# Stage b of an eight-stage float32 kernel: gate tiles taken earlier, output product with own banks, norm sums behind the first unit

## What is computed

```python
def mixer_b(h, w_in, q_gain, k_gain, w_out):        # h = rms_norm(x, g)
    proj = h @ w_in                                 # 3 patterns x (q, k, v), and z
    for g, (window, dilation) in enumerate(B_PATTERNS):
        q = apply_partial_rotary(rms_norm(qkv[:, :, 0, g], q_gain[g]), cos, sin)
        k = apply_partial_rotary(rms_norm(qkv[:, :, 1, g], k_gain[g]), cos, sin)
        o, lse = dilated_window_attention(q, k, qkv[:, :, 2, g], window // dilation, dilation)
    wgt = jax.nn.softmax(jnp.stack(lses), axis=0)
    o = jnp.einsum('gbsh,gbshd->bshd', wgt, jnp.stack(outs))
    y = o.reshape(bsz, S, B_WIDTH).astype(h.dtype) * jax.nn.silu(z)
    return y @ w_out                                # then x = x + y, and stage c begins
```

## Time and profile before

| | us |
|---|---|
| median of 3 runs | 3117.05 (3115.99 to 3117.53) |
| the profiled execution, whole | 3117.01 |
| its span, first to last instruction | 3115.2 |
| TensorE busy in it (matmul) | 2932.7 |
| VectorE busy | 1777.0 |
| ScalarE busy | 1082.4 |
| mean granted TensorE clock | 0.965 of full speed |

### The profile page before, as it was taken

The page is one execution under the profiler, slowest core; times in us unless marked ns, Lnnn a source line. Parts: engine busy times, 40 slices in busy tenths (PEclk is TensorE's granted clock), DMA queues, the critical chain, the costliest instruction groups (busy, mean ns, idle before and its releaser), DMA issues.

```text
span 3115.2 us, 38431 instructions
## 1 busy us (share of the span) xinstructions
PE 2932.7 (94%) x14024; PEld 2409.4 (77%) x14024; DVE 1777.0 (57%) x2641; ACT 1082.4 (35%) x1602; POOL 268.7 (9%) x247
## 2 busy tenths in 40 slices
PE   8999999999999899999999978699999868899998
PEld 6888888877888678878888856598888744788887
DVE  5555536763676466654545587655444578464445
ACT  4332324442444332233322444443222423442222
POOL 1000000000000000000000061220000533110001
PEclk9999999999999899999999989699999879999999
DMA  3322232212211233333232311023333210123332
GB/s 142 104 92 88 92 104 69 61 55 80 69 62 55 62 95 100 96 95 94 89 97 92 102 61 48 7 83 111 93 100 96 80 34 14 48 88 95 100 96 88
DMA packets 70400, 252.12 MB, mean 81 GB/s; under 512 B 7808, under 2 KB 9856, under 8 KB 69632
## 3 DMA queue, kind: packets, MB, share of 16 engines
q1 hardware_dynamic: 68112, 241.89, 25.0%
q10 hardware_dynamic: 2160, 8.49, 0.8%
HBM read 248.25 MB, written 2.10 MB: 80 GB/s over the span
## 4 chain that ended last, share of the span: by engine, by line
PE 77%; DVE 11%; issue 5%; ACT 3%; POOL 3%; DMA 0%; DVEq 0%; ACTq 0%; POOLq 0%
PE ps L296 17%; PE ps L297 17%; PE ps L298 17%; PE ps L570 2%; PE ps L571 2%; PE ps L572 2%; DVE w_low L283 2%; ACT w_high L276 2%; POOL arena L2014 1%; PE ps L781 1%; PE ps L783 1%; PE ps L782 1%; PE ps L854 1%; PE ps L593 1%; PE ps L840 1%
## 5 line engine op out<-in xcount | busy, mean ns | idle before, releaser
L283 DVE TENSOR_TENSOR w_low<-raw,w_high 128x1024 fp32r<-128x1024 f32 x456 | 567.0, 1248 | 417.6 <-ACT w_high L276 410.8
L296 PE MATMUL ps<-h_high,w_high 128*128 128x512 f32 x1872 | 738.0, 394 | 5.7 <-DVE arena L1423 3.0
L298 PE MATMUL ps<-h_high,w_low 128*128 128x512 f32 x1872 | 730.4, 390 | 0.0
L297 PE MATMUL ps<-h_low,w_high 128*128 128x512 f32 x1872 | 730.2, 390 | 0.0
L276 ACT ACTIVATE w_high<-raw 128x1024 fp32r<-128x1024 f32 x456 | 477.5, 1050 | 428.9 <-PE ps L298 214.1
L296 PEld LDWEIGHTS ps<-h_high,w_high 128*128 128x128 f32 x1872 | 352.6, 188 | 81.1 <-issue 4.3
L298 PEld LDWEIGHTS ps<-h_high,w_low 128*128 128x128 f32 x1872 | 352.2, 188 | 73.8
L297 PEld LDWEIGHTS ps<-h_low,w_high 128*128 128x128 f32 x1872 | 352.6, 188 | 69.9
L296 PE MATMUL ps<-y_high,w_high 128*128 128x512 f32 x656 | 258.6, 394 | 8.0 <-DVE x L520 4.3
L297 PE MATMUL ps<-y_low,w_high 128*128 128x512 f32 x656 | 257.2, 392 | 0.0
L298 PE MATMUL ps<-y_high,w_low 128*128 128x512 f32 x656 | 257.1, 392 | 0.0
(11 more groups left out here) (398 smaller groups left out, 4612.7 us busy)
## 6 DMA issues: line engine op xcount, KB each, us to landing
raw<-stream SPq DMA_DIRECT2D x456, 512.0 KB, 3.6
table<-tables_in ACTq DMA_DIRECT2D x5, 1088.0 KB, 7.3
x<-x_in ACTq DMA_DIRECT2D x8, 256.0 KB, 8.2
x_out<-x SPq DMA_DIRECT2D x16, 128.0 KB, 1.7
const<-const_in SPq DMA_DIRECT2D x1, 673.0 KB, 7.8
work<-ssm_in ACTq DMA_DIRECT2D x1, 512.0 KB, 3.5
params<-params_in ACTq DMA_DIRECT2D x1, 287.0 KB, 6.6
```

Source lines behind the costliest of these rows:

```text
L283: nc.vector.tensor_tensor(w_low[:, u.slot], raw[:, u.raw], w_high[:, u.slot].bitcast(F32), ALU.subtract).then_inc(weights_low, 1)
L296: nc.tensor.matmul(bank, wh, high[:, k], start=k == 0, stop=False)
L297: nc.tensor.matmul(bank, wh, low[:, k], start=False, stop=False)
L298: mm = nc.tensor.matmul(bank, wl, high[:, k], start=False, stop=k == tiles - 1)
```

## The change

The gate tile of head u is taken in slot (4, u) itself, after the block's negative maximum and ahead of the wait for the exponential (head 0's at the end of slot (4, 0)). gate is cut in three: gate (tanh + 1, ahead of that wait), gated (times the output, where gate was), low (y_low, at the head of the next slot, ahead of its split). ScalarE's tanh goes one slot up with it.

In the output product tiles 6 and 7 get banks 4 and 5, and no wait. k = 6 and k = 7 of a tile follow each other, so that tiles 0 to 3 are done one after another. VectorE's order there is written out: takes first, splits between, h_low behind. ScalarE splits unit 4 before the first square.

At the beginning of the stage norm_sums is issued behind values(0, 0, 0).

```diff
-        B_BANKS = (0, 1, 2, 3, 6, 7, 6, 7)
+        B_BANKS = (0, 1, 2, 3, 6, 7, 4, 5)
...
             pe.wait_ge(out_free, 8 * o + 2)
-            norm_sums(pe, R_PRE["b"], True)
...
                             values(i, g, kk)
+                        if (i, g, kk) == (0, 0, 0):
+                            norm_sums(pe, R_PRE["b"], True)
...
             for m in range(4):
                 out_tile(m, KD - 2)
-            for m in range(4):
                 out_tile(m, KD - 1).then_inc(units_done, 1)
             for m in range(4, KD):
-                if m >= 6:
-                    pe.wait_ge(out_free, 8 * o + m + 1)
                 product(pe, Unit(first + 2 * B_HALF + m), ps[:, B_BANKS[m]], y_high, y_low)
...
-                    if j == BH and 1 <= u <= BH:
-                        m = u - 1
-                        act.wait_ge(b_z_taken, BH * i + m + 1)
+                    if j == BH and u < BH:
+                        act.wait_ge(b_z_taken, BH * i + u + 1)
...
-                            act.wait_ge(b_gated, 2 * (BH * i + m))
+                            act.wait_ge(b_gated, 2 * (BH * i + u) - 1)
+                        nc.scalar.activation(b_tanh, b_szs[u % 2][:], ACT.Tanh, scale=0.5).then_inc(b_silu, 1)
+                    if j == BH and 1 <= u < BH:
+                        act.wait_ge(b_gated, 2 * (BH * i + u))
+                        nc.scalar.activation(y_high[:, 4 * i + u - 1], full[:, (u - 1) % 2], ACT.Copy).then_inc(y_high_done, 1)
...
+            for m in range(KD):
+                if m < KD - 1:
+                    split_high(act, Unit(first + 2 * B_HALF + m + 1 + AHEAD))
+                act.wait_ge(out_free, 8 * o + m + 3)
+                norm_square(act, r, m, x[:, m])
+                high_of(act, following, m)
...
+                    if j == BH and 2 <= u <= BH:
+                        low(u - 2)
                     if b_split_unit(first, i, j, u) is not None:
                         split_low(dve, b_split_unit(first, i, j, u) + AHEAD)
-                    if j == BH and 1 <= u <= BH:
...
                         nc.vector.tensor_scalar(b_neg, b_max, -1.0, None, op0=ALU.mult).then_inc(b_soft, 1)
+                        if j == BH and u < BH:
+                            take_z(u)
+                        if j == BH:
+                            gate(u - 1)
                         dve.wait_ge(b_exp, lin(n + 1, i, 16))
...
+                    if (j, u) == (BH, 0):
+                        take_z(0)
                     if j == BH and 1 <= u < BH:
                         dve.wait_ge(b_o_copied, lin(u, i, 3))
-                        gate(u - 1, b_o[:, u - 1])
+                        gated(u - 1, b_o[:, u - 1])
                 dve.wait_ge(b_pv, lin(16, i, 16))
-                gate(3, ps[:, 7])
+                gated(3, ps[:, 7])
+                low(3)
...
+            take(0)
+            split(4)
+            take(1)
+            take(2)
+            split(5)
+            take(3)
+            low_of(dve, following, 0)
+            low_of(dve, following, 1)
+            split(6)
+            low_of(dve, following, 2)
+            low_of(dve, following, 3)
+            split(7)
+            for m in range(4, KD):
+                take(m)
+                if m < KD - 1:
+                    split(m + 1 + AHEAD)
+                low_of(dve, following, m)
```

More of the change, by code:

```diff
@@ L488, in out_product, with out_split @@
             rounds(pe, last, body)
-        def out_split(act, o, first, target=None, r=None, last=False, following=None, split=0):
+        def out_split(act, o, first, target=None, r=None, last=False, following=None):
             def body(loop, at):
                 for j in range(4):
-                    if loop is not None or at + j >= split:
-                        split_high(act, Unit(first + at + j + AHEAD, loop, 4 if loop is not None else 0))
+                    split_high(act, Unit(first + at + j + AHEAD, loop, 4 if loop is not None else 0))
                     if r is not None:
@@ L500, in out_split, with out_take @@
             rounds(act, last or r is not None, body)
-        def out_take(dve, o, first, target, fresh=False, r=None, classes=False, last=False, following=None, split=0,
-                     banks=(6, 7, 6, 7, 6, 7, 6, 7)):
+        def out_take(dve, o, first, target, fresh=False, r=None, classes=False, last=False, following=None):
             def body(loop, at):
@@ L508, in body @@
                     u = Unit(first + at + j, loop, per)
-                    if loop is not None or at + j >= split:
-                        split_low(dve, u + AHEAD)
+                    split_low(dve, u + AHEAD)
                     if following is not None and at + j > 0:
@@ L515, in body @@
                     tile = target[:, bass.ds(m, 1)].rearrange("q a t -> q (a t)")
-                    bank = ps[:, banks[at + j]]
+                    bank = ps[:, 6 + j % 2]
                     if fresh:
@@ L938, in b_scalar @@
                         nc.scalar.activation(b_p, b_p, ACT.Exp, bias=b_neg, accum_out=b_sum).then_inc(b_exp, 1)
-                    if j == BH and 1 <= u <= BH:
-                        m = u - 1
-                        act.wait_ge(b_z_taken, BH * i + m + 1)
-                        if m == 0:
+                    if j == BH and u < BH:
+                        act.wait_ge(b_z_taken, BH * i + u + 1)
+                        if u == 0:
                             act.wait_ge(b_ss, 6 * BH * (i + 1))
                         else:
-                            act.wait_ge(b_gated, 2 * (BH * i + m))
-                        nc.scalar.activation(b_tanh, b_szs[m % 2][:], ACT.Tanh, scale=0.5).then_inc(b_silu, 1)
-                        if m < BH - 1:
-                            act.wait_ge(b_gated, 2 * (BH * i + m + 1))
-                            nc.scalar.activation(y_high[:, 4 * i + m], full[:, m % 2], ACT.Copy).then_inc(y_high_done, 1)
+                            act.wait_ge(b_gated, 2 * (BH * i + u) - 1)
[3 more added lines that the diff above has]
+                        nc.scalar.activation(y_high[:, 4 * i + u - 1], full[:, (u - 1) % 2], ACT.Copy).then_inc(y_high_done, 1)
                 act.wait_ge(b_gated, 2 * BH * (i + 1))
                 nc.scalar.activation(y_high[:, 4 * i + 3], full[:, 1], ACT.Copy).then_inc(y_high_done, 1)
-            out_split(act, o, first + 2 * B_HALF, x, r, last, following, split=1)
+            for m in range(KD):
[4 more added lines that the diff above has]
+                high_of(act, following, m)
         def b_vector(dve, first, o, y_base, r, last=False, following=None):
@@ L981, in gate, with take_z @@
                                             ALU.subtract).then_inc(y_low_done, 1)
+                def take_z(m):
+                    if i == 0:
+                        dve.wait_ge(b_r_kept, 1)
+                    if m == 0:
+                        dve.wait_ge(b_ss, lin(6 * BH - 1, i, 6 * BH))
+                    dve.wait_ge(units_done, b_unit(first, i, BH, m).count(1))
+                    nc.vector.tensor_tensor(b_szs[m % 2][:], ps[:, m], b_r[:], ALU.mult).then_inc(b_z_taken, 1)
                 for j, u in B_SLOTS:
@@ L1062, in b_vector, with take, split @@
                         nc.vector.tensor_copy(b_o[:, pv[0]], ps[:, 7]).then_inc(b_o_copied, 1)
+                    if (j, u) == (BH, 0):
+                        take_z(0)
                     if j == BH and 1 <= u < BH:
                         dve.wait_ge(b_o_copied, lin(u, i, 3))
-                        gate(u - 1, b_o[:, u - 1])
+                        gated(u - 1, b_o[:, u - 1])
                 dve.wait_ge(b_pv, lin(16, i, 16))
-                gate(3, ps[:, 7])
-            out_take(dve, o, first + 2 * B_HALF, x, r=r, classes=True, last=last, following=following, split=1, banks=B_BANKS)
+                gated(3, ps[:, 7])
+                low(3)
+            def take(m):
+                dve.wait_ge(units_done, Unit(first + 2 * B_HALF + m).count(1))
+                nc.vector.tensor_tensor(by_class(x[:, m]), by_class(x[:, m]), grouped(ps[:, B_BANKS[m]]),
+                                        ALU.add).then_inc(out_free, 1)
+            def split(m):
+                split_low(dve, Unit(first + 2 * B_HALF + m))
+            take(0)
[15 more added lines that the diff above has]
+                low_of(dve, following, m)
         def tail_tensor(pe, name, o, first, y_base, tiles=KD):
```

18 lines of the change are left out of this document (6 added, 12 removed).

## The result

| | before | after |
|---|---|---|
| median of 4 runs, us | 3116.52 (3114.34 to 3117.53) | 3093.41 (3087.44 to 3098.52) |
| profiled execution, us | 3117.01 | 3087.44 |
| its span, us | 3115.2 | 3085.6 |

The ratio is 0.9926, 95% interval 0.9907 to 0.9945: 23.1 us faster, where 3095.1 had been forecast. The profiled execution is the fastest of the four; 29.6 us lie between the two spans. The next table says where.

What follows compares the result with a forecast made beforehand. TensorE bounds the kernel (matmuls 94% of the span), so only its idle or low-clock time can be won. 0.5 + 9.6 + 2.5 + 9.3 = 21.9 us off 3117.0 gives 3095.1 us, range 3088 to 3103.

Steps and rivals of the forecast that it cites:

- Half 0: Stage b, half 0: the last gate tile's wait falls from 7.85 to about 1.1 us, full clock behind; 9.6 us gained.
- Half 1: Stage b, half 1: the wait for the last gate tile shortens to some 6 us, ended by w_low; 2.5 us gained.
- rival B: Half 1 restarts with the take as half 0 does, if w_low were ready: another 5.0 + 2.3, so 3088; chance 0.08.
- The wait's term: Half 1: TensorE restarts at 1021.6 against 1023.82, held by output tile 3's w_low; gain 2.2 us.
- The clock's term: Half 1: low clock stays behind the wait, slow stretch maybe 3.7 to 5.3 us; 0.3 us taken as gained.
- The end: End of stage b: waits of 2.60 and 4.28 us and their slow clock go, k = 7 waits 1.67; 9.3 gained.
- rival E: End of stage b: VectorE's written-out order makes splits fall behind TensorE, costing 29.9 us, so 3125; chance 0.04.
- The beginning: Start of stage b: moving the norm sums changes only the clock, one slow stretch behind them; 0.5 us gained.
- Rival C: Clock falls at new short waits (1.1 in half 0, 1.67 at end) and at the beginning: 5.4 back, 3100.5; chance 0.20.
- bad side: Start of stage b: slow stretches behind both the idle time and the norm sums, 1.7 + 2.4 against 2.6; 1.5 lost.
- Rival D: Half 0: take and gate delay the reciprocal and the round; 4 to 5 us lost, 3100; chance 0.08 with F.
- F: Gate tiles are still taken late; excluded for the order, counted into Rival D, together chance 0.08.

Runs made afterwards that it cites:

- e6: Changed kernel with output unit 3's weight split (high and low parts) moved one slot earlier in half 1, on ScalarE and VectorE; 3092.88 us.
- e8: Changed kernel with the edits of e5, e6 and e7 together; 3084.57 us, ratio 0.9901 to the kernel before.
- e7: Changed kernel with k = 6 of tiles 0 to 2 put ahead of k = 7 of tile 0; 3093.14 us.
- e3: Kernel before with only the new end of stage b (banks, k = 6 and 7 together, takes first, split and squares); 3106.55 us, ratio 0.9966.
- e4: Kernel before with only output tiles 6 and 7 given banks 4 and 5 and their wait removed; 3119.71 us, ratio 1.0009.
- e9: Changed kernel with the norm sums parted: 8 matmuls behind value unit 0, 8 behind unit 1; 3093.09 us.
- e10: Kernel before with stage b's norm column sums read in blocks of neighbouring positions instead of every fourth (norms go to wrong positions); 3113.31 us.
- e1: Kernel before with only the norm sums moved behind the first value unit; 3119.46 us, one execution.
- e5: Changed kernel with TensorE's order turned in half 1's slots (4, 4), (4, 5), (5, 0): both k of a tile, then the next tile; 3091.74 us.
- e11: Changed kernel with the gate tile's take and gate step put behind the softmax's scaling instead of ahead of the exponential's wait; 3100.14 us, ratio 0.9949.
- e2: Kernel before with only the gate tiles' steps in their new order; norm sums, banks and end as before; 3103.24 us, ratio 0.9958.
- after again: The changed kernel executed once more, unedited, giving its second profile; 3091.85 us, ratio 0.9924.

## Why the prediction was right, step by step

**Half 0: 9.6 said, 10.2 measured** (7.71 + 2.53 in the table). The mechanism and the new wait were right: 1.10 us, where about 1.1 had been said, and full clock behind. The gain in idle time was 0.6 low, for VectorE's and ScalarE's chain was counted too long. VectorE's timeline of the changed kernel (take, gate, reciprocal):

```profile
697.43 0.69 DVE L991 TENSOR_TENSOR root<-ps,rstd 128x512 f32<-128x512 f32 x1
698.04 0.68 DVE L971 SCALAR_TENSOR_TENSOR sq<-ssq,sq 128x512 f32<-128x512 f32 x1
698.64 0.15 DVE L1059 RECIPROCAL arena<-arena 128x1 f32<-128x1 f32 x1
```

With s = 695.06 the take starts at s + 2.37 (said 2.48) and the reciprocal at s + 3.58 (said 3.86). I added the two durations, 1.36. But steps queued on VectorE start 0.61 and 0.60 apart, 0.08 less than their duration. So the round ended earlier than counted and TensorE's wait of 0.68 for L933 vanished whole, where 0.40 had been taken off. The prediction also overlooked that L876 of round (4, 3) waited for the same copy: L872 started at 694.59, the copy ended at 695.59, L876 started at 695.64, 1.05 us behind L872; in the changed kernel it is 0.87. These two give 0.4 of the 0.6; the take's earlier place and the strips' earlier start, 0.1 each, the rest.

**Half 1: 2.5 said, 4.1 measured (3.09 + 1.02), 2.8 in the second profile.** The second wait was found rightly, with its releaser, which excludes rival B: the split starts at s + 6.61 (said 6.92), the wait is 5.87 (said some 6). e6 shows that the reason was the right one; what the Trainium skill's page "TensorE: Matmul & The Clock Gate", section Part 1, says of VectorE's strict order, weighed in the prediction, is borne out by it: the split started earlier as soon as it stood earlier in the program. VectorE's timeline of the changed kernel, with s = 1002.19:

```profile
1008.80 1.22 DVE L283 TENSOR_TENSOR w_low<-raw,w_high 128x1024 fp32r<-128x1024 f32 x1 [0.26 <-ACT w_high L276]
```

The wait's term was 0.9 low: 0.3 lie in the split's place within the round, 0.6 ahead of it, from the same causes as in half 0. What rival B took for granted, w_low ready in time, e8 brings about: there half 1 and the stretch to k = 6 take 7.1 and 8.5 us less than in the changed kernel's two profiles, where rival B had priced it at 7.3. The clock's term of 0.3 gained lies between what two profiles show behind equal waits, 1.0 gained and 0.3 lost.

**The end: 9.3 said, 9.55 measured.** With t0 = 1032.59, k = 7 restarts at t0 + 2.42 and stage c's first sums at t0 + 34.54; I had 2.42 and 34.6. The wait is 1.48 instead of 1.67. VectorE's order held, as rival E wanted it not to: the low split of unit 6 ended at t0 + 13.4 (said 13), that of unit 7 at 18.3 (17.2), the last h_low at t0 + 33.0 (32.9). The changed kernel's last two such steps:

```profile
1059.64 1.22 DVE L283 TENSOR_TENSOR w_low<-raw,w_high 128x1024 fp32r<-128x1024 f32 x1
...
1064.85 0.75 DVE L449 SCALAR_TENSOR_TENSOR h_low<-x,params,h_high 128x512 fp32r<-128x512 f32 x1 [1.31 <-ACT h_high L443]
```

e7 shows how near that last one is: with k = 7's wait gone, it is the bound. e3 shows that the end's parts win 8.9 us without the others, e4 that the banks alone win nothing.

**The beginning: 0.5 said, 1.0 in this profile, not told from nothing in all.** The slow stretch behind the sums is as taken. What I had not seen is that the start varies by 1.7 us (71.51 to 73.18) with the same code, for the idle time of 2.13 us ahead of it cost the clock in three profiles of eight. e9 and e10 show two ways to less, each in one profile: the sums in two pieces (69.99 us), and shorter sums (69.81).

**Sum.** 21.9 said, 24.9 and 23.7 measured in stage b, 23.1 by the medians: the steps' misses (+0.6, +1.6 or +0.3, +0.25, +0.5) all have one sign. The first and 0.9 of the second come from the chain counted too long; the second's other part, and the last, change with the profile. That the medians came within 1.7 us of the forecast is partly luck, as the rest of the program alone varies by 11.2 us. Rival C fell at the new waits: no clock was lost at 1.10 or 1.48 us. Its bad side at the beginning did occur, in e1, e5 and e11. What the prediction said for it, that nothing shows a single wait between 1.1 and 2.6 us, was a misreading: the kernel before has two such waits in later stages, 1.76 us at 1952.11 and 1.81 at 2627.42, without another idle time of 0.6 us or more within 8 us of them, and full clock behind. TensorE's timeline and window of the first:

```profile
1952.11 0.47 PE L1679 MATMUL ps<-h_high,w_high 128*128 128x512 f32 x1 [1.76 <-DVE full L1953]
```

```profile
1952.10:1955.10 3.00, 2.99 (x14) 2.48 (x15) 2.37 (x4) 1.48 (x2) 0.00 (x0) 1.00 0.00 0
```

This row would have borne on rival C's chance of 0.20. Rival D fell: the reciprocal slipped by 0.04 us, the round as a whole came earlier. Rivals E and F fell.

## What to carry to other kernels

A step that holds TensorE up can be put into a wait of its own engine's chain at almost no cost, if its inputs are there; count its slip by the spacing of queued steps, not by their durations. Once the wait is gone, look which other input of the same matmuls was hidden inside it (here w_low, 5.87 us), and ask of it whether data or only program order makes it late: one moved split was worth 5 us more. Here freed banks brought nothing while the engines that empty them kept their old order (e4); the wait moved, and the stretch was 0.6 us longer.

## What was not expected of the hardware

**Waits and TensorE's clock.** In stage b of the fourteen profiles, idle times of 1.10 and 1.48 us kept the clock at 1.00 (2.4 GHz) each time, and so did those of 2.20 (e3) and 2.22 (e6), each seen in one profile. Those of 2.6 ahead of output tile 4, in the five kernels with the old end (before, e1, e2, e4, e10), and of 3.06, 3.73, 3.83, 4.28, 5.87 and more, were followed by 0.50 to 0.55 (1.2 GHz). Two waits went both ways. The idle time of 2.12 to 2.16 us ahead of stage b was followed directly by 1.2 GHz in four profiles (e1, e2, e5, e11) and not in the other ten, so the single profiles of 2.20 and 2.22 don't show that such a wait is safe. And stage c has an idle time of 2.97 to 3.01 us, followed by slow matmuls in seven profiles (before, e1, e2, e6, e7, e10, after again) and not in the other seven. TensorE's timeline and window, first of the changed kernel, then of the kernel before:

```profile
1100.19 0.50 PE L296 MATMUL ps<-h_high,w_high 128*128 128x512 f32 x1 [2.97 <-DVE arena L1459]
```

```profile
1100.20:1103.60 3.40, 3.40 (x15) 2.83 (x16) 1.81 (x2) 1.55 (x2) 0.00 (x0) 1.00 0.52 154
```

```profile
1124.55 0.66 PE L296 MATMUL ps<-h_high,w_high 128*128 128x512 f32 x1 [2.99 <-DVE arena L1423]
```

```profile
1124.50:1128.00 3.50, 3.45 (x9) 2.68 (x10) 1.82 (x2) 1.58 (x3) 0.00 (x0) 0.53 0.51 150
```

**Equal waits, unequal cost.** Behind half 1's wait the slow matmuls last 3.15 us in the first profile of the changed kernel (wait 5.87) and 5.9 in the second (wait 5.88). The granted clock is at 0.50 for the same 6.8 us in both; the windows of the first and the second profile:

```profile
1006.40:1013.20 6.80, 3.12 (x7) 2.48 (x8) 2.67 (x4) 1.73 (x3) 0.00 (x0) 0.50 0.26 73
```

```profile
1008.60:1015.40 6.80, 5.88 (x14) 4.63 (x15) 0.86 (x1) 0.00 (x0) 0.00 (x0) 0.50 0.28 80
```

What differs is where it lies: the clock falls 2.2 us after TensorE's last matmul in the first (1004.20) and 5.0 us after it in the second (1003.64), so 3.7 of the 6.8 us pass while TensorE stands idle in the first, and 0.9 in the second. Half of the difference in slow work, (5.88 - 3.12) / 2 = 1.4 us, is what the stretch to k = 6 differs by (23.80 - 22.51 = 1.3). So what such a wait costs here is not told by the length of the low clock, but by the work that TensorE does in it. In the kernel before, too, the clock is at 0.50 for 10.2 us around the end of the wait of 7.85 us (701.5 to 711.7), and 4.8 of them are idle time.

**The spread of the rest.** The same sum explains it. Over all stretches of low clock behind stage b, TensorE is busy for 113.1 us in the changed kernel's first profile and for 135.0 in e6. Half of the difference is 11.0 us, and their rests differ by 11.2. Over the fourteen profiles, half of this busy time plus TensorE's idle time follows the rest with a correlation of 0.99. Between the first two profiles most of the 5.3 us lie in stage o: from its norm sums to those of the last stage it is 285.9 us before and 280.4 after.
